# Up projections of a gated FFN in pairs of blocks: seven quarter products for eight, and three chunk groups

## What is computed

```python
def conv_ffn(h, buf, w_up, w_dw, b_dw, w_down):
    g, val = jnp.split(h @ w_up, 2, axis=-1)
    g, tail = causal_depthwise_conv(g, buf, w_dw, b_dw)
    return (jax.nn.gelu(g) * val) @ w_down, tail
```

## Time and profile before

| | |
|---|---|
| median of 3 runs | 1453.63 us (1453.62 to 1454.96) |
| time of the profiled execution | 1458.59 us |
| its span | 1457.0 us, 28796 instructions |
| busy share | PE 98%, PEld 91%, DVE 67%, ACT 62%, POOL 19% |
| mean granted clock of TensorE | 0.995 |
| chain that ended last, by engine | PE 85%, DVE 8%, ACT 2%, issue 2% |
| matmul line 749 in that chain | 70% |

### The profile page before, as it was taken

One profiled execution on the slowest core, in us unless ns is written; L12 is line 12 of the kernel. 1 busy time (PEld: TensorE's weight loads), 2 busy tenths in 40 slices (PEclk: granted clock), 3 DMA queues, 4 the chain that ended last, 5 costly groups with the idle time before them and its releaser, 6 DMA issues.

```text
span 1457.0 us, 28796 instructions
## 1 busy us (share of the span) xinstructions
PE 1424.4 (98%) x11346; PEld 1321.6 (91%) x11346; DVE 981.4 (67%) x1443; ACT 906.4 (62%) x1743; POOL 275.6 (19%) x440
## 2 busy tenths in 40 slices
PE   5999999999999999999999999999999999999998
PEld 4877758999999999999989976679999999999997
DVE  4889975887754688743736557865878744867633
ACT  4699977767644677643625557865877643765543
POOL 2499820000000232200000032210000000322200
PEclk9999999999999999999999999999999999999999
DMA  9888684255554455554426557864355554454652
GB/s 378 316 295 295 242 284 137 82 179 162 173 187 159 145 160 173 177 185 147 150 72 212 178 202 258 307 230 126 107 167 165 188 180 136 159 171 163 198 166 99
DMA packets 72119, 273.53 MB, mean 188 GB/s; under 512 B 8064, under 2 KB 10128, under 8 KB 71600
## 3 DMA queue, kind: packets, MB, share of 16 engines
q1 hardware_dynamic: 65824, 247.69, 50.1%
q0 software_dynamic: 5872, 23.64, 4.7%
q10 hardware_dynamic: 288, 0.35, 0.1%
HBM read 262.80 MB, written 8.85 MB: 186 GB/s over the span
## 4 chain that ended last, share of the span: by engine, by line
PE 85%; DVE 8%; ACT 2%; issue 2%; DMA 1%; POOL 1%; POOLq 0%; DVEq 0%; SPq 0%; ACTq 0%
PE ps L749 70%; DVE ps L1936 4%; PE ps L1014 3%; PE ps L724 2%; PE ps L1073 1%; PE ps L1110 1%; PE ps L1171 1%; PE ps L1132 1%; PE ps L1148 1%; PE ps L819 1%; DVE y L1956 1%; PE ps L929 1%; PE ps L853 1%; PE ps L1023 1%; ACT s_prod L1380 1%
## 5 line engine op out<-in xcount | busy, mean ns | idle before, releaser
L1767 DVE TENSOR_TENSOR w_lo<-raw,w_hi 128x1024 fp32r<-128x1024 f32 (+1 forms) x296 | 387.4, 1310 | 224.6 <-ACT w_hi L1285 224.1
L749 PE MATMUL ps<-h_hi,w_hi 128*128 128x288 f32 x1920 | 525.2, 297 | 1.7 <-DVE h_lo L1841 1.7
L749 PE MATMUL ps<-h_lo,w_hi 128*128 128x288 f32 x1920 | 519.3, 295 | 0.0
L1285 ACT ACTIVATE w_hi<-raw 128x1024 fp32r<-128x1024 f32 (+1 forms) x309 | 347.2, 1124 | 103.0 <-PE ps L749 72.0
L749 PEld LDWEIGHTS ps<-h_hi,w_hi 128*128 128x128 f32 x1920 | 360.3, 188 | 8.2 <-DVE h_lo L1841 4.5
L749 PEld LDWEIGHTS ps<-h_lo,w_hi 128*128 128x128 f32 x1920 | 360.0, 188 | 1.1 <-issue 0.2
L749 PE MATMUL ps<-h_hi,w_lo 128*128 128x288 f32 x1920 | 312.8, 294 | 0.1
L749 PEld LDWEIGHTS ps<-h_hi,w_lo 128*128 128x128 f32 x1920 | 274.4, 188 | 0.4 <-DVE w_lo L1767 0.4
L749 PE MATMUL ps<-act_pair,w_hi 128*128 128x288 f32 x1408 | 207.0, 295 | 0.0
L749 PEld LDWEIGHTS ps<-act_pair,w_hi 128*128 128x128 f32 x1408 | 194.4, 188 | 0.0
L2118 DVE SCALAR_TENSOR_TENSOR cv<-g_pad,par,cv 128x224 f32<-128x224 f32 (+1 forms) x176 | 85.4, 485 | 46.0 <-ACT cv L1543 41.0
(11 more groups left out here) (241 smaller groups left out, 1928.0 us busy)
## 6 DMA issues: line engine op xcount, KB each, us to landing
raw<-w_k_dram SPq DMA_DIRECT2D x245, 512.0 KB, 3.5
raw<-w_down_dram SPq DMA_DIRECT2D x64, 704.0 KB, 4.1
ada_w<-w_ada_dram SPq DMA_DIRECT2D x71, 512.0 KB, 6.0
k_page<-cache_kt_dram SPq DMA_DIRECT2D x32, 512.0 KB, 5.3
v_page<-cache_v_dram POOLq DMA_DIRECT2D x32, 512.0 KB, 5.2
ada_h<-w_ada_dram SPq DMA_DIRECT2D x7, 512.0 KB, 6.2
ada_u<-w_ada_dram SPq DMA_DIRECT2D x6, 512.0 KB, 15.0
ada_g<-w_ada_dram SPq DMA_DIRECT2D x6, 512.0 KB, 5.7
```

Of the source, the lines that this page charges most:

```text
L749: return pe.matmul(ps[:, BANK[b], 0:HALF], lhsT=w[s][:, kb * P:(kb + 1) * P], rhs=v[:, at, :] if down else v[:, at, lo:hi], start=(at == 0 ...
L1285: act.activation(w_hi[SLOT[n]][:, 0:cols], raw[s][:, 0:cols], ACT.Copy).then_inc(s_hi, 1)
L1767: dve.tensor_tensor(w_lo[s][:, 0:cols], raw[n % RING][:, 0:cols], w_hi[s][:, 0:cols].bitcast(F32), ALU.subtract).then_inc(s_lo, 1)
```

## The change

The first four chunks (`PLAIN`) stay as they are, half 0 and then half 1. The other 18 of a layer are **pairs**: gate and value block of a chunk with both token halves. The 1024 input features are cut in two, so a pair is a 2x2 matrix of weights (gate G0 G1, value V0 V1, each 4 pieces) times a 2x2 matrix of h (feature half, token half). In place of eight quarter products of 12 matmuls it takes seven, by Strassen's scheme. Products 1 to 4 use h itself, 5 to 7 three differences of its quarters (`t_op`, by `sum_of_h` on GpSimd, `t_round` on ScalarE, `t_low` on VectorE). The weights of 5, 6, 7 and 3 are sums and differences that GpSimd makes for each pair (`weight_sums`: V0+V1, less G0, G0-V0, and G1 less the second). Each product's weight, 128x512, is rounded (`combo_round`) and gets a low part (`combo_low`) in a half of a ring slot; six are in flight. The order of products is 1, 5, 3 of the pair before, 6, 4 of the pair before, 2, 7. Partial results are copied between PSUM banks and added (`keep_one`, `keep_five`, `keep_two`, `drain_first` on ScalarE, `add_five_seven` and `drain_last` on VectorE); taps, gelu, product and rows of `act_pair` then run over all 576 tokens at once.

The chunks go in **three groups** of 7, 7 and 8 (3, 7 and 8 pairs), each followed by its part of all 16 down blocks. Parts 0 and 1 are copied out to y, and parts 1 and 2 begin by bringing that back to PSUM (`bring_back`). A down weight serves both halves in a row. For groups 0 and 1 two down blocks stand ahead of the last two products, all rows but the last, and two behind them; for the third group two and one.

There is room for four `raw` tiles of 1024 columns, two a pair. The chains of `a_out`, `o` and layer 0's FFN are all tight; that of half 1 of `a_out` and `o` makes its norm at the seventh block behind its end, within the eight blocks of half 0. GpSimd adds a shift to y and takes the differences of h (`add_shift`, `sum_of_h`) during the four chunks of half 1.

```diff
-FH = FC // 2
+PLAIN = 4
+PART_CHUNKS = (7, 7, 8)
+PART_AT = (0, 7, 14)
+PARTS = len(PART_CHUNKS)
+ACT_ROWS = max(PART_CHUNKS)
...
         for h in range(2):
-            for i in range(FC):
+            for i in range(PLAIN):
                 for s in range(2):
                     out.append(Block("up", layer, 2 * i + s, h, 0, C, row + 2 * i + s, 2 * i + s))
-            for n in range(C):
-                for part in range(2):
-                    out.append(Block("down", layer, n, h, part, FH, (2 * layer + part) * C + n, n))
-
-    up, down = list(range(C)), list(range(C))[::-1]
+        for g, k in enumerate(PART_CHUNKS):
+            if g < PARTS - 1:
+                order = [(n, h, n) for n in range(C) for h in range(2)]
+            else:
+                order = [(n, 0, n) for n in up] + [(n, 1, pos) for pos, n in enumerate(down)]
+            for n, h, pos in order:
+                out.append(Block("down", layer, n, h, g, k, (PARTS * layer + g) * C + n, pos))
...
+def _products(count):
+    out = []
+    for j in range(count):
+        out += [(1, j), (5, j)] + [(3, j - 1)] * (j > 0) + [(6, j)] + [(4, j - 1)] * (j > 0) + [(2, j), (7, j)]
+    return out + [(3, count - 1), (4, count - 1)]
...
-CHAINS = [_chain(0, 0, 2, "a_out", 0, True), _chain(0, 1, 2, "a_out", 0, False)._replace(y_stat=0),
-          _chain(1, 0, 3, "down", 0, False), _chain(1, 1, 3, "down", 0, True),
-          _chain(2, 0, 5, "o", 0, True), _chain(2, 1, 5, "o", 0, False)._replace(y_stat=0),
+    return Chain(r, half, norm, ended, 2, (3, 4, 5, 6), (4, 5, 6, 7), (5, 6, 7, 8), 10, 11, False)
+CHAINS = [_chain(0, 0, 2, "a_out", 0, True), _chain(0, 1, 2, "a_out", 0, True),
+          _chain(1, 0, 3, "down", 0, True), _chain(1, 1, 3, "down", 0, True),
+          _chain(2, 0, 5, "o", 0, True), _chain(2, 1, 5, "o", 0, True),
           _chain(3, 0, None, "down", 1, False), _chain(3, 1, None, "down", 1, False)]
 N_CHAINS = len(CHAINS)
+STAT_INSIDE = (0, 1, 2, 4, 5)
...
+            def pair_weights(gid, j):
+                i = PART_AT[gid % PARTS] + j + (PLAIN if gid % PARTS == 0 else 0)
+                row = BLOCKS[(UP0, UP1)[gid // PARTS]].row + 2 * i
+                for s, t in enumerate(pair_tiles(gid, j)):
+                    if j >= 2:
...
+                    sp.dma_start(raw[t][:], w_k8[row + s]).then_inc(pair_in[t], 16)
...
+            def product(gid, q):
...
+                else:
+                    pe.wait_ge(both_added, m + 1)
+                if role in T_ORDER:
+                    pe.wait_ge(t_lo, T_LO_FROM + 4 * layer + T_ORDER.index(role) + 1)
+                pe.wait_ge(combo_lo, 7 * PAIR_FROM[gid] + q + 1)
...
+            def down_part(gid):
...
+                for b in blocks[:ahead[0]]:
+                    one_half(b, lambda kb: down_ready(b, kb), kbs=range(k - 1))
+                product(gid, end - 2)
+                product(gid, end - 1)
+                for b in blocks[ahead[0]:]:
+                    one_half(b, kbs=range(k - 1))
...
+            def combo_round(gid, q):
...
+                if role in (1, 2, 4):
+                    s = int(role == 4)
+                    act.wait_ge(pair_in[pair_tiles(gid, j)[s]], pair_arrived(gid, j, s))
+                else:
+                    act.wait_ge(sum_made, sums_needed(role, m))
+                act.activation(hi, combo_source(gid, q), ACT.Copy).then_inc(combo_hi, 1)
...
+            def pair_group(gid):
+                order, m0, count = PRODUCTS[gid], PAIR_FROM[gid], PAIR_COUNT[gid]
+                first, end = GROUP_LOAD[gid], 7 * PAIR_COUNT[gid]
+                for q in range(1, end):
+                    (done, i), (role, j) = order[q - 1], order[q]
+                    if done == 1:
+                        keep_one(gid, i, m0 + i)
+                    elif done == 5:
+                        keep_five(gid, i, m0 + i)
+                    elif done == 6:
+                        keep_two(gid, i, m0 + i)
+                    elif done == 2:
+                        drain_first(gid, i, m0 + i)
+                    if COMBOS <= q + COMBOS - 1 < end:
+                        combo_round(gid, q + COMBOS - 1)
+                    if q == COMBOS and gid % PARTS == 0:
+                        t_round(gid // PARTS, 3)
+                    if j and role == 6:
+                        last_tap(gid, j - 1, m0 + j - 1)
+                    elif j and role == 2:
+                        pair_gate(gid, j - 1, m0 + j - 1)
+                    elif j and role == 7:
+                        pair_hi_row(gid, j - 1, m0 + j - 1)
+                    if q == end - 4:
+                        split(first)
...
+            def pair_group(gid):
+                order, m0, count = PRODUCTS[gid], PAIR_FROM[gid], PAIR_COUNT[gid]
+                first, end = GROUP_LOAD[gid], 7 * PAIR_COUNT[gid]
+                for q in range(1, end):
+                    (done, i), (role, j) = order[q - 1], order[q]
+                    if done == 7:
+                        add_five_seven(gid, i, m0 + i)
+                        if i:
+                            pair_low_row(gid, i - 1, m0 + i - 1)
+                    elif done == 3:
+                        drain_last(gid, i, m0 + i)
+                    if COMBOS <= q + COMBOS - 1 < end:
+                        combo_low(gid, q + COMBOS - 1)
+                    if q == COMBOS and gid % PARTS == 0:
+                        t_low(gid // PARTS, 3)
+                    if role == 4 and j < count - 1:
+                        pair_taps(gid, j, m0 + j)
+                    elif j and role == 7:
+                        pair_product(gid, j - 1, m0 + j - 1)
...
+            def weight_sums(gid, j):
+                m = PAIR_FROM[gid] + j
+                gate_w, value_w = pair_raw(gid, j)
+                low, high = slice(0, QUARTER), slice(QUARTER, 2 * QUARTER)
+                for s in range(2):
+                    pool.wait_ge(pair_in[pair_tiles(gid, j)[s]], pair_arrived(gid, j, s))
+                if m % LAYER_PAIRS == 0:
+                    norm = (2, 5)[gid // PARTS]
+                    pool.wait_ge(h_ready, STEP[norm, C - 1, 1] + 1)
+                if m:
+                    pool.wait_ge(combo_lo, PRODUCT_AT[5, m - 1] + 1)
+                pool.tensor_tensor(s_sum[0][:], value_w[:, low], value_w[:, high], ALU.add).then_inc(sum_made, 1)
+                if m:
+                    pool.wait_ge(combo_lo, PRODUCT_AT[6, m - 1] + 1)
+                pool.wait_ge(sum_made, 4 * m + 1)
+                pool.tensor_tensor(s_sum[1][:], s_sum[0][:], gate_w[:, low], ALU.subtract).then_inc(sum_made, 1)
+                pool.tensor_tensor(value_w[:, low], gate_w[:, low], value_w[:, low], ALU.subtract).then_inc(sum_made, 1)
+                pool.wait_ge(combo_lo, PRODUCT_AT[1, m] + 1)
+                pool.wait_ge(sum_made, 4 * m + 3)
+                pool.tensor_tensor(gate_w[:, low], gate_w[:, high], s_sum[1][:], ALU.subtract).then_inc(sum_made, 1)
...
+                for g in range(PARTS):
+                    gid = PARTS * layer + g
+                    weight_sums(gid, 0)
+                    if g == 0:
+                        sum_of_h(layer, 3)
+                    for j in range(PAIR_COUNT[gid]):
+                        m = PAIR_FROM[gid] + j
+                        if j + 1 < PAIR_COUNT[gid]:
+                            weight_sums(gid, j + 1)
+                        if m % LAYER_PAIRS:
+                            keep_tail(m - 1)
+                        set_edge(m)
```

610 lines of the change are left out of this document (485 added, 125 removed).

## The result

The changed kernel takes **1582.94 us** (median of 4 runs, 1579.91 to 1586.55), a ratio of 1.088 to the kernel before (95% interval 1.086 to 1.090). The kernel before took 1453.62 to 1454.96 us in three executions; a fourth took 3266.63 us and is left out. Slower was forecast, but the time lies 83 us above the forecast and 38 above the range (1435 to 1545). The profiled execution took 1579.91 us, its span 1578.3, so 121.3 us more span than before.

What follows compares the result with a forecast made beforehand. TensorE was taken to bound the kernel before, and a loop of waits among the other engines the pairs after. -57.3 + 62 + 24 + 6 + 8 + 4 = +46.7 on 1458.6 gave 1505.3, less 5.0: 1500 us, range 1435 to 1545.

Steps and rivals of the forecast that it cites:

- The gain: TensorE in the pairs: 84 matmuls for 96, 18 pairs in each of two layers, -57.3 us.
- The pair loop: Pairs: waits through the value tile's load take 12.5 us, 14.2 with VectorE-GpSimd contention, against TensorE's 11.13; +62 us.
- The hindrance: In a pair, VectorE and GpSimd steps reading SBUF block each other: 1.7 us a pair, bounds 0 and 2.7.
- The forecast's high end: All terms at their high ends, with a pair period of 15.4 us: +90 us, so 1543 us.
- The start: Start of each FFN: chain and norm within half 0's blocks, +24 us for two layers; product 5 late in half 1, +6.
- The group ends: After a group's last pair: about 7.5 us of steps, 6.4 covered, 2.8 for a block in the third group; +8 us.
- The keys: Keys of layer 0: the norm ahead comes at once, 1.05 us a chunk against TensorE's 0.4; +4 us (0 to 6).
- Rival (c): TensorE's clock falls in the new gaps, half of 18 gaps, +36 us on top: 1536 us; chance 0.11.
- Rival (a): Pairs: TensorE stays the bound, loop under 11.13 us, only group ends and keys remain: 1408 us; chance 0.17.

Runs made afterwards that it cites:

- floor: Changed kernel with ScalarE's rounding for product 4 ahead of gelu and gate copy, GpSimd's h steps and weight sums and VectorE's half-1 chain narrowed: 1460.1 us.
- third_weight: Changed kernel, but behind product 4 of the third group the third down block takes all rows but the last from the second block's weight: 1586.6 us.
- keep_warm: Changed kernel plus 90 extra matmuls into a free bank ahead of the wait for product 1 of each FFN's first pair: 1589.2 us.
- all_moved: Changed kernel, rounding for product 4 ahead of gelu and gate copy, y's shift on ScalarE, h differences and weight sums on VectorE: 1514.2 us, 1.0408 of before.

## Why the prediction was wrong

**The gain, right.** 432 matmuls at 0.1325 us went, and the other engines, not TensorE, set the pace of the pairs: 13.85 us for TensorE's 11.13.

**The pair loop, right in size, wrong in mechanism.** The step that fails is "The value tile of pair c+2 can be loaded only when product 4 of pair c has its low part [...] Together 12.5 us a pair and no shorter". Without loads the period is 13.96. The two queues' zigzag is 11.94 us bare and 13.85 with the sums; the load's path ends within 0.3 us of it (rounding of the sum done at 484.0, gate sum at 484.26), shares its steps from the last tap to the low for product 4, and hid it. The sum lacked the zigzag's other steps, which run beside the load and end last: product, row rounding, low row, three lows, gate sum. So the forecast's 14.2 is near 13.85 in part by luck: a wrong path that is nearly as long. The hindrance, put at 1.7 us a pair, is right in mechanism and is 1.9. (The forecast's high end takes a period of 15.4, where 12.5 + 2.7 is 15.2; that is 3 us of the range and decides nothing.) The pairs cost 84.1 - 14.6 = 69.5 us for 62; 14.6 is what TensorE waited ahead of the six first down blocks.

**The start, wrong by 39 us, the largest miss.** The chain in half 0 was 24 for two layers and is 29: half 1 begins 14.7 and 14.3 us later than six blocks without a wait behind the first gate copy. What failed is the step behind it, 6 us for half 1 in the forecast and 40 measured (19.6 and 20.6 a layer): "The first sum comes about 23 us after the first gate block [...] +6 us". It counts GpSimd's time in half 1 and leaves VectorE's as it was, although the hindrance of the earlier trace rows stands a few lines above. The first sum starts at 343.99, 26 us behind the first gate copy of half 1, and its low is a step in a queue of VectorE that is late. By the timeline VectorE's steps between 317 and 355 us are 17.7 us longer than the same steps alone. Narrow steps on GpSimd give back 12.3 to 13.1 a layer, narrow chain steps 5.7 to 6.1, narrow sums 4.4 to 5.3; with all three the start is 12 a layer, for 15 in the forecast. In those 12 TensorE waits 2.3, 3.3 and 2.8 us in layer 0; no run takes these apart.

**The group ends, wrong by 36 us** (29.4 in the table and the 14.6 above, for 8). About 7.5 us against 6.4 that cover them was close for the first two groups (0.65 us of wait each); for the third it is 7.3 against 4.4. Not forecast were three things. The first down blocks of a group wait for a row or a bank that comes from the loop (14.6 us): they are the loop's lateness, and in floor those waits sum to 4.2. A gap of 3.3 us ahead of line 944, since the chain of layer 0's FFN is now tight. And the clock behind the gaps, 0.69 from 697 to 704 us: of the 29.4 us of the ends 16.1 are waits of TensorE, and some 10 are work at half clock, an estimate from the granted clock of the stretches. What would shorten the ends stays open: third_weight did not, and floor still has 25.6.

**The keys, right in sign, half in size.** 4 us were put there; from the end of layer 0's FFN to line 1334 it is 167.8 us for 165.7, 2.1 more, and 1.9 of it is one wait ahead of line 950, for y_sum. That the stages outside the FFNs are 4 us shorter in all comes from elsewhere. From TensorE's wait for line 1171 (now 1410) to its next one it was 89.9 us and is 85.3: the profiled execution before ran at half clock from 870 to 878 us, this one at 1.00 behind the same wait, though that is as long (2.0 us for 1.8). So the clock fell in one execution and not in the other, and the 4.6 us belong to that execution before and not to the change; they are near the 5.0 by which the other executions before were shorter.

**Rival (c), the clock**: right that it falls, which the forecast's sum put at nothing ("clock at 1.00"), wrong on the price in the loop. In layer 0's second group it fell in every second pair (0.88 for 1.00) with the same 13.85 us: TensorE is busy 12.98 instead of 11.43 us and waits 0.9 instead of 2.4. In layer 1's second group it stayed at 1.00, and the period is 13.86. By the granted clock TensorE loses some 12 us in the starts, 13 in the pairs and 10 in the ends, an estimate as above. The 10 are most likely a price, since TensorE is the bound again there at once; of the 12 the part in the first pair is none (keep_warm), and the rest no run takes apart. The Trainium skill, page "TensorE: Matmul & The Clock Gate", section "HAM oscillation — how this bites in real kernels", says that idle gaps between bursts of matmuls make the clock fall again and again and that this costs time: the trace agrees as to the fall, and in the pairs not as to the time.

**The hindrance** was used too narrowly: it stands in the pair's sum and not in the start's. The Trainium skill, page "SBUF — State Buffer", section "Who interferes with whom", says that a VectorE instruction with two inputs in SBUF and a GpSimd instruction that reads SBUF contend, and that the order of issue decides who waits: the lines above agree (VectorE steps of 0.45 us that take 2.93 and 2.73 beside GpSimd's).

**Rival (a)** would have needed a loop below 11.13 us, and no kernel that computes everything had one.

## What to carry to other kernels

Before a cheaper algorithm is judged by TensorE's count, write the other engines' lists over one period as one closed path and look for every loop in it, not the first that has the right length; then test it by taking out a link, since here a move of two instructions on ScalarE was worth 40 us and the removal of the loads from a group's third pair on nothing. When wide work goes to GpSimd, price it by what it adds to VectorE's steps beside it, in every stage, and try it on VectorE too. A wait that a profile names is where a loop shows: take it away and see whether the period changes.

## What I had not expected of the hardware

A GpSimd step of 1152 elements (line 2886, 3.0 us on average) makes a VectorE step of 64 columns take 2.63 us instead of 0.28, and the same differences on VectorE take 1.35 us each (all_moved). A wide step takes about half as long on VectorE as on GpSimd (1.35 for 2.7 us with 1152 elements, 0.69 for 1.3 with 512), so work moved to the idle engine took longer there and held up VectorE as well. And TensorE at 1.2 GHz for part of a pair left the period unchanged.
